# Turning h on VectorE in the routed jobs of a mixture-of-experts layer, with the weight copies moved to ScalarE and GpSimd

## The reference

```python
xn = rms_norm(x, ffn_norm_w)
# 64 experts, 8 of them per token (sigmoid router, limited to 4 of 8 groups), weights w_tok,e
y_e(t) = (silu(xn[t] @ w_gate[e]) * (xn[t] @ w_up[e])) @ w_down[e]      # 1024 -> 256 -> 1024
out[t] = x[t] + sum_e w[t,e] * y_e(t) + shared_swiglu(xn[t])            # the shared expert: all tokens
```

## Time and profile before

| | before |
|---|---|
| median of 3 runs | 1434.14 us (1434.01 to 1435.91) |
| the profiled execution, its own time | 1430.39 us |
| span of its trace | 1428.5 us |
| busy PE, DVE, ACT, POOL | 1403.0, 804.3, 442.1, 687.1 us |
| data moved by DMA, mean rate | 330.07 MB, 231 GB/s |

### The profile page before, as it was taken

The page is one execution under the profiler, slowest core; times in us unless marked ns, Lnnn a source line. Parts: engine busy times, 40 slices in busy tenths (PEclk is TensorE's granted clock), DMA queues, the critical chain, the costliest instruction groups (busy, mean ns, idle before and its releaser), DMA issues.

```text
span 1428.5 us, 23051 instructions
## 1 busy us (share of the span) xinstructions
PE 1403.0 (98%) x6057; PEld 584.4 (41%) x6058; DVE 804.3 (56%) x1057; ACT 442.1 (31%) x648; POOL 687.1 (48%) x713
## 2 busy tenths in 40 slices
PE   7999999999999989999999999999999999999998
PEld 3456565565566433333333333333333333333333
DVE  2334453544444567666666676676676676666622
ACT  1223323233234212333333333333333333333330
POOL 3010313313122545666666666666667665666631
PEclk9999999999999999999999999999999999999999
DMA  9411102112019439999999999898999999999937
GB/s 344 186 66 63 48 34 82 45 37 82 14 57 380 163 118 339 318 293 359 283 369 327 331 289 327 250 280 267 306 342 380 326 329 300 308 332 275 345 43 209
DMA packets 76029, 330.07 MB, mean 231 GB/s; under 512 B 16007, under 2 KB 17544, under 8 KB 50324
## 3 DMA queue, kind: packets, MB, share of 16 engines
q1 hardware_dynamic: 45140, 249.62, 45.6%
q0 software_dynamic: 30848, 79.94, 24.2%
HBM read 282.74 MB, written 65.11 MB: 244 GB/s over the span
## 4 chain that ended last, share of the span: by engine, by line
PE 92%; DMA 4%; issue 2%; DVE 1%; POOL 1%; ACT 0%; SPq 0%; ACTq 0%; POOLq 0%; DVEq 0%
PE psP L743 57%; PE psW L743 31%; PE psW L956 2%; DMA area<-x_dram 2%; DMA wts<-in_w_in_dram 1%; PE psW L794 1%; POOL slot_table L624 1%; PE psT L836 0%; PE psT L751 0%; PE psT L820 0%; DMA tabT<-slot_table,jobrow_i 0%; PE psW L771 0%; DMA area<-xn_dram,rows_i 0%; DMA x_dram<-area,sidx 0%; DVE bias L1628 0%
## 5 line engine op out<-in xcount | busy, mean ns | idle before, releaser
L743 PE MATMUL psP<-wts,bias 128*64 (+1 forms) x1296 | 575.7, 597 | 4.9 <-DVE bias L1628 3.6
L743 PE MATMUL psP<-area,bias 128*64 128x512 f32 x1264 | 561.0, 597 | 0.0
L743 PE MATMUL psW<-wts,area 128*64 (+2 forms) x1592 | 426.3, 593 | 2.2 <-ACT wts L1259 1.6
L1628 DVE STREAM_TRANSPOSE bias<-area 64x512 f32<-64x512 f32 x316 | 347.7, 1100 | 4.8 <-DMA area<-xn_dram,rows_i 1.5
L698 POOL DMA_INDIRECT out_dram<-area,sidx x79 | 236.7, 2996 | 187.0 <-ACT area L1251 110.4
L743 PEld LDWEIGHTS psP<-wts,bias 128*64 128x64 f32 (+1 forms) x1296 | 172.8, 138 | 342.1 <-issue 342.0
L743 PE MATMUL psP<-wts,area 128*128 128x512 f32 (+1 forms) x704 | 287.7, 560 | 6.2 <-DMA wts<-in_w_in_dram 4.9
L743 PEld LDWEIGHTS psW<-wts,area 128*64 128x64 f32 (+1 forms) x1592 | 150.3, 148 | 251.0 <-issue 248.9
L1637 DVE SCALAR_TENSOR_TENSOR dsq<-dsq,area,psP 128x256 f32<-128x256 f32 x79 | 53.5, 677 | 279.4 <-ACT dsq L1231 276.0
L674 POOL DMA_INDIRECT area<-xn_dram,gidx x150 | 155.9, 1039 | 93.0 <-POOL gidx L670 65.4
L743 PEld LDWEIGHTS psP<-wts,area 128*128 128x128 f32 x704 | 131.2, 192 | 136.2 <-issue 126.1
(11 more groups left out here) (227 smaller groups left out, 805.4 us busy)
## 6 DMA issues: line engine op xcount, KB each, us to landing
wts<-in_w_exp_gate_dram SPq DMA_DIRECT2D x64, 1024.0 KB
wts<-in_w_exp_up_dram SPq DMA_DIRECT2D x64, 1024.0 KB
wts<-in_w_exp_down_dram SPq DMA_DIRECT2D x64, 1024.0 KB
wts<-in_w_in_dram SPq DMA_DIRECT2D x4, 2048.0 KB, 18.0
area<-in_x_dram SPq DMA_DIRECT2D x8, 512.0 KB
wts<-in_w_out_dram SPq DMA_DIRECT2D x1, 4096.0 KB, 18.3
area<-u_dram SPq DMA_DIRECT2D x16, 256.0 KB, 2.9
xn_dram<-area POOLq DMA_DIRECT2D x16, 256.0 KB
```

What stands on the lines that cost most here:

```text
L743: return nc.tensor.matmul(out_, lhsT, rhs, start=start, stop=stop)
L1628: i = V.transpose(xT[par][u * HB:(u + 1) * HB, :, b * HB:(b + 1) * HB] .rearrange("p k (g t) -> p g k t", g=2), rows[:, u])
```

## The change

- The turned h of a routed job no longer comes from TensorE. VectorE's new `turn_h` transposes it in 32 x 32 blocks, 16 instructions, from `hh` straight into `hT[1 - par]`, which now has two buffers in the routed jobs too. `t_h` and `read_h` are left out there.
- The copy of B's gate/up weights moves from VectorE to ScalarE, behind `read_y` of the job before.
- The copy of B's down weights moves from ScalarE to GpSimd, between `gather(j + 4)` and `scatter(j)`.
- TensorE's gate/up now waits for the multiply of h two jobs back (`s_h_ready`) instead of its turning; the multiply waits for the turning of the job before (`s_hT_ready`) instead of TensorE's transposes.
- The ends of the loops are rewritten to match.

```diff
@@ gpsimd
+            def copy_dn(r):
+                e = pool.value_load(ringB_i[0:1, bass.ds(r, 1)], min_val=1, max_val=NE)
+                pool.wait_ge(s_down, r + NSH)
+                for sl in range(NSLOT):
+                    loads = (e + (NSLOT - sl)) // NSLOT
+                    pool.wait_ge(dn_ld[sl], (loads + (1 >> loads)) * 16)
+                nc.gpsimd.tensor_copy(dn_b, wts[:, bass.ds((e % NSLOT) * SLOTW + 2 * GUW, FT * D)]).then_inc(s_dn_copy, 1)
...
                     gather(j + 4, k, i * 6 + 3 * k)
+                    copy_dn(i * 2 + (k + 1))
                     scatter(j, k, i * 6 + (1 + 3 * k))
...
@@ tensor
             def gate_up_halves(j, par, w0):
                 pe.wait_ge(s_xT_ready, j - (NSH - 1))
-                pe.wait_ge(s_hT_ready, j - 1)
+                pe.wait_ge(s_h_ready, j - 1)
                 pe.wait_ge(s_gu_copy, j - (NSH - 1))
...
                     gate_up_halves(r + NSH, k, (now % NSLOT) * SLOTW)
-                    down_halves(r + NSH - 1, (was % NSLOT) * SLOTW)
-                    t_h(r + NSH, psW[:, 0, :])
+                    down_halves(r + NSH - 1, 1 - k, (was % NSLOT) * SLOTW)
...
@@ scalar
-            def copy_dn(r):
-                e = act.value_load(ringB_i[0:1, bass.ds(r, 1)], min_val=1, max_val=NE)
-                act.wait_ge(s_down, r + NSH)
+            def expert_b(r):
+                return act.value_load(ringB_i[0:1, bass.ds(r, 1)], min_val=1, max_val=NE)
+
+            def copy_gu(r, par, e):
                 for sl in range(NSLOT):
                     loads = (e + (NSLOT - sl)) // NSLOT
-                    act.wait_ge(dn_ld[sl], (loads + (1 >> loads)) * 16)
-                A(dn_b, wts[:, bass.ds((e % NSLOT) * SLOTW + 2 * GUW, FT * D)], ACT.Copy).then_inc(s_dn_copy, 1)
+                    act.wait_ge(gu_ld[sl], (loads + (1 >> loads)) * 32)
+                act.wait_ge(s_gu, r + (NSH - 1))
+                A(gu_b[par].rearrange("p m k f -> p (m k f)"), wts[:, bass.ds((e % NSLOT) * SLOTW, 2 * GUW)], ACT.Copy) \
+                    .then_inc(s_gu_copy, 1)
...
                 for k in ks:
-                    j = i * 2 + (NSH + 2 + k)
-                    silu(j, k)
-                    read_y(j - 1, 1 - k, False)
-                    read_h(j)
-                    copy_dn(i * 2 + (2 + k))
...
+                    r = i * 2 + (2 + k)
+                    silu(r + NSH, k)
+                    read_y(r + (NSH - 1), 1 - k, False)
+                    copy_gu(r + 2, k, expert_b(r + 2))
...
@@ vector
-            def h_mul(j, par, w):
+            def h_mul(j, par, w, shared=0):
 
                 dve.wait_ge(s_silu, j + 1)
-                if not (isinstance(j, int) and j == 0):
-                    dve.wait_ge(s_th, j)
+                if shared:
+                    dve.wait_ge(s_th, shared)
+                elif not (isinstance(j, int) and j == 0):
+                    dve.wait_ge(s_hT_ready, j)
...
+            def turn_h(j, par):
+                dve.wait_ge(s_h_ready, j + 1)
+                dve.wait_ge(s_down, j - 1)
+                for q in range(P // QUAD):
+                    for t in range(P // QUAD):
+                        i = V.transpose(hT[1 - par][q * QUAD:(q + 1) * QUAD, :, t * QUAD:(t + 1) * QUAD],
+                                        hh[t * QUAD:(t + 1) * QUAD].rearrange("t (f q p) -> t q f p", f=FT, p=QUAD)[:, q])
+                i.then_inc(s_hT_ready, 1)
...
                     h_mul(r + NSH, k, tab_w[:, bass.ds(r, 1)])
+                    turn_h(r + NSH, k)
                     turn_x(r + (NSH + 2), k, i + 3)
-                    copy_gu(r + 2, k)
```

More of the change, by code:

```diff
@@ L711, in _ @@
             pool.wait_ge(s_n_jobs, 4)
+            copy_dn(0)
             def jobs(i, ks):
@@ L722, in last_jobs @@
                 for m in range(4):
+                    if m < 3:
+                        copy_dn(n_less_4 + (m + 1))
                     scatter(n_less_4 + (NSH + m), (par + m) % 2, n_less_4 * 3 + (2 * m))
@@ L894, in step, with gate_up_late @@
                 out_project(T, 1)
-            def gate_up_late(t, ks):
+            def gate_up_late(n, t, ks):
                 buf, ld = shared_place(NSH + t)
@@ L900, in gate_up_late @@
                     pe.wait_ge(gu_ld[LATE_SLOT], 32 * LATE_LOADS)
-                    if t >= 2:
+                    if t == 0:
+                        pe.wait_ge(s_h_ready, n + NSH)
+                    elif t >= 2:
                         pe.wait_ge(s_hT_ready, n + (NSH + t - 1))
@@ L951, in gate_up_halves, with t_h @@
                 i.then_inc(s_gu, 1)
-            def t_h(j, to):
+            def t_h(j):
                 pe.wait_ge(s_h_ready, j + 1)
                 for f in range(FT):
-                    i = nc.tensor.transpose(to[:, f * P:(f + 1) * P], hh[:, f * P:(f + 1) * P], ident[:, :])
+                    i = nc.tensor.transpose(psP[:, side(j), f * P:(f + 1) * P], hh[:, f * P:(f + 1) * P], ident[:, :])
                 i.then_inc(s_th, 1)
@@ L1009, in _ @@
             gate_up(1, range(3, 4))
-            t_h(0, psP[:, side(0), :])
+            t_h(0)
             t_y(TL)
@@ L1021, in _ @@
             gate_up(2, range(5, KT))
-            t_h(1, psP[:, side(1), :])
+            t_h(1)
             pe.wait_ge(s_x1_ready, NT)
@@ L1039, in _ @@
             mm(psW[0:JMAX, 1, 258:260], ended[:, JT:JT + JMAX], nb2[:, :], True, True).then_inc(s_post_pe, 1)
-            t_h(2, psP[:, side(2), :])
+            t_h(2)
             down(1)
@@ L1055, in _ @@
             i.then_inc(s_tab_t, 1)
-            t_h(3, psP[:, side(3), :])
+            t_h(3)
             down(2)
-            t_h(4, psP[:, side(4), :])
+            t_h(4)
             down(3)
@@ L1234, in read_h @@
                 act.wait_ge(s_th, j + 1)
[L1235 to L1241, removed]
+                if j >= 2:
+                    act.wait_ge(s_down, j - 1)
+                A(hT[1 - side(j)].rearrange("p f n -> p (f n)"), psP[:, side(j), 0:FE], ACT.Copy).then_inc(s_hT_ready, 1)
             def read_y(j, par, static):
@@ L1698, in _ @@
             xn_scale(TL)
-            h_mul(1, side(1), one_col[:, 0:1])
+            h_mul(1, side(1), one_col[:, 0:1], 1)
             route(TL)
@@ L1711, in _ @@
             V.tensor_copy(nb_row[:, :], bc(nb2[:, 1:2], [NE, P])).then_inc(s_post, 1)
-            h_mul(2, side(2), one_col[:, 0:1])
+            h_mul(2, side(2), one_col[:, 0:1], 2)
             read_shared(0, side(0))
@@ L1758, in _ @@
             dve.wait_ge(s_post_pe, 5)
-            h_mul(3, side(3), one_col[:, 0:1])
+            h_mul(3, side(3), one_col[:, 0:1], 3)
             dve.wait_ge(s_gu, 3)
@@ L1765, in _ @@
             read_tab()
-            h_mul(4, side(4), one_col[:, 0:1])
+            h_mul(4, side(4), one_col[:, 0:1], 4)
             read_shared(2, side(2))
@@ L1808, in _ @@
             for t in range(NLATE):
-                h_mul(less_2 + (NSH + 2 + t), t % 2, one_col[:, 0:1])
+                h_mul(less_2 + (NSH + 2 + t), t % 2, one_col[:, 0:1], NSH + t if t else 0)
                 if t:
```

56 lines of the change are left out of this document (32 added, 24 removed).

## The result

| | before | after |
|---|---|---|
| median | 1435.03 us (1434.01 to 1436.10, 4 runs) | 1398.41 us (1395.92 to 1399.11, 4 runs) |
| the profiled execution, its own time | 1430.39 us | 1398.12 us |
| span of its trace | 1428.5 us | 1396.4 us |
| start of the first routed job, of the last | 526.7, 1373.8 us | 531.3, 1341.3 us |

The ratio is 0.9742, with a 95% interval of 0.9725 to 0.9759: 2.6% faster, 36.6 us. The forecast was 1396 us.

A forecast was written before the change was run, and what follows sets the result against it. TensorE was taken to bound the routed jobs. 79 x (10.82 - 10.35) = 37 us plus 1 at the end, 38 us off 1430.39, gave 1392.4; with 3.75 us to the median, 1396 us. Range 1388 to 1440 us.

The forecast's parts named there:

- What bounds the kernel: Routed jobs: TensorE sets the time of a job, 10.82 us, of which 24 matmul pairs take 10.29 us.
- The gain per job: TensorE in the routed jobs: two transposes of h removed, 0.53 us in each of 79 jobs, 42 us.
- VectorE: Routed jobs: loses the gate/up copy, gains 16 small transposes; 8.7 us a job, bounds 7.4 and 9.8, below 10.29.
- ScalarE: Routed jobs: gate/up copy at most 3.84 us, 6.2 us a job, 4 us of cover, silu not delayed.
- GpSimd: Routed jobs: serial chain 7.96 us plus down copy 2.0 and 0.3 before it, 10.3 us, the same as TensorE's.
- The end: Last down matmul: its 1.60 us wait for ScalarE's copy shrinks as GpSimd starts it at once, about 1 us less.
- The sum: Whole kernel: period 10.35 us saves 37 us, plus 1 at the end: 38 us; 1392.4 profiled, 1396 us median.
- (1): Clean: GpSimd under 10.2 us, DMAs keep up, period 10.29, 1391 us; chance 0.48 together with the forecast.
- (2): GpSimd binds routed jobs mildly, period 10.45 to 10.8 us: 1404 to 1432, middle 1418 us; chance 0.20.
- (3): GpSimd's down copy and what precedes it exceed 2.86 us, TensorE waits every job: slower, 1440 to 1524 us; chance 0.18.
- (4): Weight loads bind where experts have two blocks; some 20 jobs keep 10.82 us, 10 us more: 1401 to 1407; chance 0.10.
- (5): TensorE's transposes cost nothing, since it would wait there anyway: no change; chance 0.04.

The follow-up runs named there:

- the run with one copy moved: Kernel before, with only the gate/up weight copy moved from VectorE to ScalarE, behind the down copy; TensorE keeps its two transposes: 1443.74 us, ratio 1.0075.
- the longer chain: Kernel after, with a second GpSimd copy of 128 x 512, its data unused, between the down copy and the scatter: 1417.42 us, ratio 0.9886.

## Why the prediction was right, step by step

- **What bounds the kernel**: right. 10.30 us a job after, worked out as 24 x 0.429 = 10.29, and putting the two transposes back gives 10.82 again.
- **The gain per job**: right, 0.52 us. For the period that I took for the sum, 10.35, the mean in the profile after is 10.30 + 6.6 / 78 = 10.38, and 10.37 in the second. But it is a long first period and a few late jobs, and not an even excess from two queues of the same length; that the size of this allowance fitted was luck.
- **VectorE**: a small transpose was taken at 0.225 us and takes 0.236, at a pitch of 0.249; sixteen take 3.98 us, not 3.6. Turning x rose from 1100 to 1118 ns. Its sum, in the timeline of the kernel after:

```profile
893.84 0.67 DVE L1661 SCALAR_TENSOR_TENSOR dsq<-dsq,area,psP 128x256 f32<-128x256 f32 x1 [1.23 <-ACT dsq L1248]
894.64 3.98 DVE L1671 STREAM_TRANSPOSE area<-dsq 32x64 f32<-32x64 f32 x16
898.65 4.50 DVE L1650 STREAM_TRANSPOSE bias<-area 64x512 f32<-64x512 f32 x4
```

  It ends at 903.15, 9.3 us after it began, and not 8.7: inside the bounds of 7.4 to 9.8, and it stays under 10.30. The estimate of 0.224 us from the Trainium skill's fixed latency (VectorE: DVE Perf Modes, "The TRN2 errata — SBUF-src ops pay a fixed extra latency per instruction") was 10% short of the pitch; its advice against such short instructions holds as a price, but the price fitted.
- **ScalarE**: the copy was taken at no more than 3.84 us and takes 3.62. From reading y to the end of the silu's turn it needs 1.0 + 1.3 + 3.6 + 0.4 = 6.3 us, forecast 6.2. Silu was not delayed. What a delayed silu can cost where TensorE waits for h of the same job, the run with one copy moved shows: 0.42 us at every fourth job.
- **GpSimd**: the scatter to `out` fell from a mean of 3 us to 1485 ns in all 79 jobs, taken at 1.43 us. The copy takes 1.89 us for 2.0 taken, 0.17 us in front of it for 0.3, and the remainder of the chain 7.99 for 7.96. The chain is 10.05 and not 10.3 us, so it doesn't set the pace, but its slack is 0.25 us. The sentence "the same as TensorE's" was wrong by that quarter, and on the safe side. GpSimd's irregular pauses of up to 2.5 us, which with so little slack reach TensorE, were not in the sum of its chain, though the trace of before has them. The figure for two inputs of the Trainium skill (GPSIMD Engine Reference, "3.1 Elementwise — side-by-side cycle accounting"), 4.5 us for 2048 elements, is not the price of a copy: with one input the trace has 1.89. The rule of "4.1 Engine selection" on the same page, one input at roughly line rate, is the one that the trace bears out.
- **The end**: the wait of the last down fell from 1.60 to 0.82 us as forecast, but the tail didn't get shorter (54.7 and 55.1 us):

```profile
1355.34 3.65 PE L756 MATMUL psW<-wts,area 128*64 x16 [0.82 <-POOL wts L692]
```

  GpSimd's last down copy, at 1353.24, stands ahead of the scatter at 1356.33, the next scatter waits for that one to land, and the merge of `x1_dram` behind it takes back what TensorE gained. The forecast's 1 us isn't there.
- **The sum**: 38 us forecast, 36.6 measured, 37.2 the second time. So the mechanism was right, and the last microsecond of the agreement is luck: the allowance for uneven jobs fitted for another reason than the one given, and the end gave nothing. The step from the profiled execution to the median, +3.75 us, was only arithmetic when it was made; the second profile of before, 3.6 us longer, has it in the start of the jobs, 526.7 against 530.4 us.
- **The rivals**: (1), clean, had the condition that GpSimd's chain is under 10.2 us. It is 10.05, and still the kernel took 1396 to 1398 us and not 1391: the average chain was the wrong condition, for the pauses need slack too. Clean is the kernel with both copies on ScalarE, 1391.51 us. (2), GpSimd binding mildly, begins 0.3 us further on, and the longer chain at 1417 us sits in the middle of its range. (3) needed 2.86 us for copy and gap, and they take 2.06. (4), the transfers: ScalarE's copy waits for loads in 54 jobs, 60.3 us in all, but never longer than 1.4 us, a part of which is the register work ahead of the copy, and TensorE behind it not once. The DMA share over the jobs (560 to 1340 us) is 0.95, 0.96 before: the transfers kept up with the shorter job. (5) fell with the transposes put back.

## What to carry to other kernels

Where one engine is full, count only what leaves its queue, and for every engine that takes the work write down the chain of one round and its slack against the new, shorter round: here VectorE had 1.0 us, ScalarE 4 us and GpSimd 0.25 us, and the copy on the engine with the least slack cost 4.7 us that the engine with the most took for nothing. An operation that is placed ahead of a short one (a copy before silu) costs from the moment at which it makes that one late by more than the lead of the full engine's program, here 0.13 us at the loop's edge, even where no data is late. And irregular pauses need slack of their own: with 0.25 us left they reached TensorE, with the copy elsewhere they didn't. Look at more than one execution before you explain a few microseconds: the start of the jobs moved by 3.7 us between two executions of the same program.

## What the runs showed of the hardware

- GpSimd's copy of float32: 128x2048 in 1.89 us and 128x512 in 0.60, so (1.89 - 0.60) / 1536 = 0.84 ns an element and 0.17 us fixed. VectorE does 128x4096 in 2.29 us, 0.56 ns an element, and ScalarE in 3.62.
- A float32 copy of VectorE stretches small work of GpSimd beside it: an index copy of 64 elements took 2.24 instead of 0.18 us, the descriptors of a scatter a mean of 3.0 instead of 1.49. VectorE's copy itself stayed at 2.29 us beside these, and took 2.75 to 3.19 (900 to 1270 us of the kernel with its copy left on VectorE) where GpSimd also had its 128x2048 copy.
- TensorE's array can run dry with all data there and every other engine waiting. Its program needed 2.35 us from the last wait, over the loop's branch and two register loads, to the first matmul; where that wait was released 0.55 us later than the 2.48 us ahead of before, 0.42 us were lost at each trip.
- Two executions of one program had their routed jobs start 3.7 us apart (526.7 and 530.4 us), which is all of the 3.6 us between their times.
